# Gate and up blocks of both feed-forward layers: high and low activations in one product of 512 columns

## The chip, the cores and the metric

One core of one Trainium2 chip runs the whole program. The metric is the device time of one execution in microseconds (us). The core has a matrix engine (TensorE; PE in the profile, PEld its weight loads), a vector engine (VectorE, DVE), a scalar engine (ScalarE, ACT), a queue for transfers (SyncE, SP) and eight accumulation banks of 128x512 float32 values (PSUM) that only TensorE's products fill and that VectorE and ScalarE read out.

## The reference, cut to what matters

Two transformer blocks over 256 tokens of width 1024. The second one has two feed-forward layers of this form, with D_FF = 2816:

```
def swiglu(x, w_gate, w_up, w_down):
    return (jax.nn.silu(x @ w_gate) * (x @ w_up)) @ w_down

h = h + 0.5 * swiglu(rms_norm(h, ffn1_norm[i]), ffn1_w_gate[i], ffn1_w_up[i], ffn1_w_down[i])
...
h = h + 0.5 * swiglu(rms_norm(h, ffn2_norm[i]), ffn2_w_gate[i], ffn2_w_up[i], ffn2_w_down[i])
```

Everything else (the first block with its expert layer, the attention and retention branches of the second, the last gate) is not touched by the change.

## The kernel before, in words

All data is float32, but TensorE is fed rounded numbers of the type fp32r. So each operand is held as a high part and a low part: `wh` and `wl` for weights, `hh` and `hl` for activations (`yh` and `yl` for the activations of the down products). A product of two such operands is three matmuls (`mm3`, line 529): high times high, then the low activations against the high weights, then the high activations against the low weights, all added up in the same bank. The weights are the stationary operand and 256 tokens are the moving one.

The weights come in chunks of 128x2048 values (1 MB), each in two units of 128x1024. ScalarE makes the high part of a unit (`wh`, line 1233), VectorE the low part (`wl`, line 1803). There are six slots for units (`NU`), so a unit may be split once TensorE has used the one six units before it. Both engines split a fixed distance ahead of the work (`AHEAD` = 4 units, in the helper `ahead`), and do it in the order of their written-out programs.

Each feed-forward layer runs over eleven column blocks i of 256. Called g, u and d here, they go over TensorE in the order g0 u0 g1 f1a u1 g2 u2 d0 d1 g3 u3 d2 ... g10 u10 d9 d10 in the first layer (`f1a` is a sum for a norm) and g0 u0 s2 g1 u1 d0 g2 u2 d1 ... in the second (`s2` is such a sum too). A block g, u or d is 16 triples of matmuls. g and u each fill one bank (`lin_fm`); the two 128x256 halves of the bank are two groups of 128 columns m. d adds into banks 4 to 7 over all i (`down_fm`).

On VectorE, `ffn_act` (line 2253) multiplies g by the token scale `rs` out of its bank (L2257), waits for ScalarE's silu (L1521), multiplies with u out of its bank (L2262), multiplies by the scale once more (L2264); ScalarE rounds the result to `yh` (L1507), VectorE makes `yl` (L1823). Both engines then split further weights.

Which bank a result goes to is fixed beforehand by a table (`job`, `over`, `fixed_to`). `take` on TensorE waits until every earlier result of that bank has been read out:

```
        def take(pe, name):
            p, b, n = jobs[name]
            if n:
                pe.wait_ge(bank_out[p][b], n)
            return BK[b]
```

In the first layer g0 is in bank 4, u0 in 5, `f1a` in 3, and g1, u1, g2, u2, g3, ... take the banks 0, 1, 2, 3, 0, ... in turn. In the second layer g0, u0, g1, u1, ... take the banks 0, 1, 2, 0, ... in turn, and `s2` is in bank 3.

Between the blocks VectorE has other work of its own in the first layer: the scales out of `f1a` ahead of `ffn_act(0)`, a norm (`first_normed`, L2296) after `ffn_act(4)`, and the tables of angles (`rope_tables`, L2300 to L2319) ahead of `ffn_act(5)`, for which ScalarE takes two sines (L1552, L1554).

Of the kernel before, what the change touches and what calls it, by code (L numbers as in the profile page):

```python
# [12 lines left out]
def offsets(pairs):  # L13
# [13 lines left out]
ohe rank tm tm_h flag pg g32 moe  # L27
g_gx g_gc g_pt g_s g_tr g_d g_yh g_sc
hn_h f1x f1_s f1_t f1_yh f1_yl f1_yb tab
rot rope ix_mm ix_sel sco  # L30
rs_mm rv_mm rm_mm rm_sq rvar yn
at_mm at_m at_e at_d at_tr at_v at_yh
iw_t av_t sgy rg_l mg mg_h mg_l
# [19 lines left out]
    "unscaled_l": [("f1_l", 8), ("mx_l", 8), ("f2_l", 8), ("pl_l", 8)],  # L53
    "gated_h": [("rg_h", 4), ("gain", 8)],
    "norm_t": [("n2_t", 8), ("hn_t", 8)],
}


# [3 lines left out]
def program(nc, D, out):  # L62
# [5 lines left out]
    ALU, ACT, AX = mybir.AluOpType, mybir.ActivationFunctionType, mybir.AxisListType  # L68
    cx = ExitStack()

    with cx:
# [16 lines left out]
        def S(name):  # L88
            return sems[name]

        def nth(name, n):
            return sems[name], base[name] + n
# [5 lines left out]
        RAW = [sb(f"raw{i}", [128, 2048]) for i in range(NR)]  # L98
        with ExitStack() as outer:
            ob = lambda name, n: outer.enter_context(nc.sbuf_tensor(name, [128, n], f32r))  # L100
            HHt, HLt = ob("hh", 4096), ob("hl", 4096)
            WH = [ob(f"wh{i}", 1024) for i in range(NU)]
            WL = [ob(f"wl{i}", 1024) for i in range(NU)]
        XGt = []
# [9 lines left out]
        wide = lambda T: T[:, :].rearrange("p (k t) -> p k t", k=8)  # L114
        half = lambda T, i: T[:, 2048 * i:2048 * i + 2048].rearrange("p (k t) -> p k t", k=8)
        HW, LW = wide(HHt), wide(HLt)
        HX, LX = HW[:, :, 0:256], LW[:, :, 0:256]
        HC, LC = HW[:, :, 256:512], LW[:, :, 256:512]
        H0, L0, H1, L1 = half(HHt, 0), half(HLt, 0), half(HHt, 1), half(HLt, 1)
        YH, YHA = YHt[:, 0:2048].rearrange("p (k t) -> p k t", k=8), YHt[:, 2048:3072].rearrange("p (k t) -> p k t", k=4)  # L120
        YL, YLA = YLt[:, 1024:3072].rearrange("p (k t) -> p k t", k=8), YLt[:, 0:1024].rearrange("p (k t) -> p k t", k=4)
# [20 lines left out]
        two = lambda b: b[:, :].rearrange("p (k t) -> p k t", k=2)  # L142
# [103 lines left out]
        chunks, where = [], {}  # L246
# [122 lines left out]
        def done(e, name, i=0):  # L369
            e.wait_ge(*nth("used", units_used(2 * where[name, i] + 1)))  # L370

        jobs, uses = {}, {"": [0] * 8, "g_": [0] * 8, "d_": [0] * 8}
# [6 lines left out]
        def over(pool, p=""):  # L379
            at = [0]  # L380

            def put(*names):
                for n in names:
                    job(n, pool[at[0] % len(pool)], p)
                    at[0] += 1
            return put
# [12 lines left out]
        def fixed_to(banks, *names):  # L399
            fixed(*zip(names, banks))  # L400
# [10 lines left out]
        rot = over([5, 6, 7], "g_")  # L411
# [28 lines left out]
        rot = over([0, 1, 2, 3])  # L440
        job(("f1", "g", 0), 4)
        job(("f1", "u", 0), 5)
        job("f1a", 3)
        for i in range(1, 11):
            rot(("f1", "g", i), ("f1", "u", i))
        for i in range(4):
            job(("f1", "y", i), 4 + i)
        put = over(ALL7)
# [33 lines left out]
        put = over(ALL7)  # L482
        job("s2", 3)
        put(*[("wo2", i) for i in range(4)])
        rot = over([0, 1, 2])
        for i in range(11):
            rot(("f2", "g", i), ("f2", "u", i))
        for i in range(4):
            job(("f2", "y", i), 4 + i)
        put = over(ALL7)  # L490
# [6 lines left out]

        def bank(name):
            return BK[jobs[name][1]]

        def copied(name):
            p, b, n = jobs[name]
            return bank_out[p][b]

        def evicted(e, name):
            p, b, n = jobs[name]
            e.wait_ge(bank_out[p][b], n + 1)
# [7 lines that stand above are left out]
        def tensor_program(pe):  # L515
# [18 lines left out]
            def lin_fm(c, outs, xh, xl, ready=None, nk=8, ncols=256, N=256, between=None):  # L534
                per, hk = 512 // N, nk // 2
                for u in range(2):
                    if u and between:
                        between()
                    h, l = weights(2 * where[c] + u, hk)
                    for m in range(ncols // 128):  # L540
                        o = outs[m // per][:, (m % per) * N:(m % per) * N + N]
                        for k in range(hk):
                            x = u * hk + k
                            if ready and m == 0:
                                pe.wait_ge(*nth(ready[0], ready[1][x]))
                            t = mm3(o, h[:, k, m * 128:(m + 1) * 128], l[:, k, m * 128:(m + 1) * 128], xh[:, x, :], xl[:, x, :],
                                    x == 0 and m % per == 0, x == nk - 1)
                    t.then_inc(S("used"), 1)

            def lin_tm(c, outs, ntt, xh, xl, ready=None, ncols=256):  # L550
# [29 lines left out]
            up_to = list(range(1, 9))  # L580
# [26 lines left out]
            for x in range(2):  # L607
                b = take(pe, ("cb", x))
                for k in range(4):
                    t = mm(b[:, k * 128:k * 128 + 128], CV[:, 4 * x + k, 0:1].broadcast_to([128, 128]), ident, k == 0, True)  # L610
                t.then_inc(S("cb"), 1)
            ada_rows(0)
            b = take(pe, "statx")
# [5 lines left out]
            b = take(pe, "statc")  # L619
# [25 lines left out]
            for j in range(4):  # L645
                b = take(pe, ("dec", j))
# [145 lines left out]
            b = take(pe, "w_stat")  # L792
# [4 lines left out]
            b = take(pe, "router")  # L797
            arrived(pe, where["w_r", 0])
            w = RAW[raw_of[where["w_r", 0]]][:, 0:288].rearrange("p (k n) -> p k n", k=8)
            for k in range(8):  # L800
                pe.wait_ge(*nth("n2_h", k + 1))
                for x in range(2):
                    t = mm(b[:, 256 * x:256 * x + 36], H2F[:, k, 128 * x:128 * x + 128], w[:, k, :], k == 0 and x == 0, k == 7)
            t.then_inc(S("used"), 2)
            for x in range(2):
                for q in range(2):
                    b = take(pe, ("tm", x, q))
                    for k in range(4):
                        t = pe.transpose(b[:, k * 128:(k + 1) * 128], H2F[:, 4 * q + k, x * 128:x * 128 + 128], ident)
                    t.then_inc(S("tm"), 1)  # L810
            b = take(pe, "rank")
# [207 lines left out]
            b = take(pe, "f1a")  # L1019
# [3 lines left out]
            mm(b[:, 256:512], ones, ACCB, False, True).then_inc(S("f1a_mm"), 1)  # L1023
            lin_fm(("f1u", 1), [take(pe, ("f1", "u", 1))], H0, L0)
            for i in range(2, 11):
                lin_fm(("f1g", i), [take(pe, ("f1", "g", i))], H0, L0)
                lin_fm(("f1u", i), [take(pe, ("f1", "u", i))], H0, L0)
                if i == 2:
                    down_fm("f1", "f1d", 0, 11, ("f1_yl", "f1_yb"))
                down_fm("f1", "f1d", i - 1, 11, ("f1_yl", "f1_yb"))  # L1030
# [135 lines left out]
                lin_fm(("w_out2", i), [take(pe, ("wo2", i))], H0, L0, ("mg_l", [1, 1, 2, 2, 3, 3, 4, 4]) if i == 0 else None)  # L1166

            for i in range(11):
                lin_fm(("f2g", i), [take(pe, ("f2", "g", i))], H1, L1, ("f2_l", up_to) if i == 0 else None)
                lin_fm(("f2u", i), [take(pe, ("f2", "u", i))], H1, L1)  # L1170
                if i == 0:
                    stat_sum("s2", "s2_acc", "s2_mm")
                else:
                    down_fm("f2", "f2d", i - 1, 11, ("f2_yl", "f2_yb"))
# [13 lines left out]
            for m in range(2):  # L1188
                f = slice(m * 128, m * 128 + 128)
                b = take(pe, ("pg", 3 + m))  # L1190
# [28 lines left out]
        def scalar_program(a):  # L1219
# [282 lines left out]
            def split_act(i, P, dn, ready, T):  # L1502
                ready()
                if i >= 2:
                    done(a, dn, i - 2)
                y = 4 * (i % 2)
                a.activation(YH[:, y:y + 2, :], T[i % 2], ACT.Copy).then_inc(S(P + "_yh"), 1)  # L1507
# [9 lines left out]
            assert at[0] == after  # L1517

            def silu_scaled(i, P, G):
                evicted(a, (P, "g", i))  # L1520
                a.activation(G[i % 2], G[i % 2], ACT.Silu).then_inc(S(P + "_s"), 1)  # L1521

            def ffn_act(i, P, dn, G, T):
                silu_scaled(i, P, G)
                split_act(i, P, dn, lambda: a.wait_ge(*nth(P + "_t", i + 1)), T)

            through("f1u", 0)
# [263 lines left out]
        def vector_program(v):  # L1791
# [23 lines left out]
            def step(ins):  # L1815
                ins.then_inc(S(own[0]), 1)
                own[1] += 1

            def prev():
                v.wait_ge(*nth(own[0], own[1]))  # L1820
# [430 lines left out]
            assert at[0] == after and own[1] == stepped  # L2251

            def ffn_act(i, P, G, T, rs, g, u):
                done(v, g, i)
                if i >= 2:
                    evicted(v, (P, "u", i - 2))
                v.tensor_tensor(G[i % 2], two(bank((P, "g", i))), rs, ALU.mult).then_inc(copied((P, "g", i)), 1)  # L2257
                v.wait_ge(*nth(P + "_s", i + 1))
                done(v, u, i)
                if i >= 2:  # L2260
                    v.wait_ge(*nth(P + "_yl", i - 1))
                v.tensor_tensor(T[i % 2], G[i % 2], two(bank((P, "u", i))), ALU.mult).then_inc(copied((P, "u", i)), 1)  # L2262
                evicted(v, (P, "u", i))
                v.tensor_tensor(T[i % 2], T[i % 2], rs, ALU.mult).then_inc(S(P + "_t"), 1)  # L2264
                low_act(i, P, T)

# [521 lines left out]
```

## Time and profile before

| | |
|---|---|
| median of 3 runs | 1176.04 us (1169.3 to 1182.11) |
| the profiled execution | 1174.52 us, of which the span of instructions is 1172.6 us |
| granted TensorE clock, mean | 0.971 |
| busy: TensorE, weight loads | 1101.8 us (94%), 937.3 us (80%) |
| busy: VectorE, ScalarE | 709.0 us (60%), 519.4 us (44%) |

The shares are means over the whole span, over stages with different limits. A matmul's record covers its whole way through the array, so that records overlap: the distance from start to start is what one costs in a stream. PEclk of 1.00 is the full clock of 2.4 GHz, 0.50 is 1.2 GHz.

### The profile page before, as it was taken

The numbers are of one execution on the slowest core, as the hardware profiler recorded it, in microseconds if no ns is written. First come the engines' busy times: TensorE is split into PE (matmuls) and PEld (weight loads), VectorE is DVE, ScalarE is ACT, GpSimd is POOL, SyncE is SP. The second block draws the span as 40 slices with busy tenths as digits, with TensorE's granted clock in tenths as the row PEclk, the third lists the DMA queues.
The fourth block names the chain that finished last, engine by engine and source line by source line (L and its number), as shares of the span: only waits on it lengthen the run. The fifth ranks groups of instructions, "written<-read, shape, count | busy, mean of one in ns | idle before, by whom it ended". The sixth has DMA issues, their size and how long they took to land.

```text
span 1172.6 us, 18961 instructions
## 1 busy us (share of the span) xinstructions
PE 1101.8 (94%) x7908; PEld 937.3 (80%) x7908; DVE 709.0 (60%) x1125; ACT 519.4 (44%) x797; POOL 0.2 (0%) x4
## 2 busy tenths in 40 slices
PE   5899997899999998999999989978999999999997
PEld 3689876545555554999999988877889999999996
DVE  1879777423332335876756789767645776555667
ACT  3674223211111113654434576358854554443455
POOL 0000000000000000000000000000000000000000
PEclk9899997799999999999999999988999999999998
DMA  9945617999999947465454433432345545545321
GB/s 384 379 164 216 252 60 292 388 422 413 408 410 406 407 189 325 146 246 182 180 205 162 148 108 125 146 108 73 108 144 203 197 168 202 182 173 201 134 98 36
DMA packets 38153, 257.72 MB, mean 220 GB/s; under 512 B 4368, under 2 KB 5264, under 8 KB 7856
## 3 DMA queue, kind: packets, MB, share of 16 engines
q1 hardware_dynamic: 36720, 252.38, 56.4%
q10 hardware_dynamic: 1344, 4.08, 0.9%
q8 instruction: 65, 1.06, 0.4%
q14 instruction: 24, 0.20, 0.0%
HBM read 255.39 MB, written 1.05 MB: 219 GB/s over the span
## 4 chain that ended last, share of the span: by engine, by line
PE 67%; DVE 11%; ACT 5%; issue 2%; DVEq 0%; ACTq 0%
PE bank L527 66%; DVE wl L1803 3%; ACT wh L1233 2%; DVE rstd L1827 1%; DVE xt L1853 1%; ACT arena L1578 1%; DVE acc L1865 1%; DVE hl L1870 0%; PE bank L903 0%; ACT L1243 0%; ACT arena L1243 0%; PE bank L861 0%; DVE tn L1885 0%; DVE arena L2021 0%; ACT rstd L1247 0%
## 5 line engine op out<-in xcount | busy, mean ns | idle before, releaser
L527 PE MATMUL bank<-hh,wh 128*128 128x256 f32 (+2 forms) x1256 | 365.0, 291 | 9.6 <-DVE hl L1823 4.3
L527 PE MATMUL bank<-hl,wh 128*128 128x256 f32 (+2 forms) x1256 | 360.4, 287 | 0.0
L527 PE MATMUL bank<-hh,wl 128*128 128x256 f32 (+2 forms) x1256 | 360.1, 287 | 0.0
L1803 DVE TENSOR_TENSOR wl<-raw,wh 128x1024 fp32r<-128x1024 f32 (+4 forms) x238 | 267.7, 1164 | 82.6 <-ACT wh L1233 79.2
L1233 ACT ACTIVATE wh<-raw 128x1024 fp32r<-128x1024 f32 (+4 forms) x238 | 227.9, 1003 | 71.3 <-PE bank L527 71.2
L527 PEld LDWEIGHTS bank<-hh,wh 128*128 128x128 f32 (+1 forms) x1256 | 242.5, 193 | 18.9 <-issue 13.6
L527 PEld LDWEIGHTS bank<-hl,wh 128*128 128x128 f32 (+1 forms) x1256 | 242.7, 193 | 1.3
L527 PEld LDWEIGHTS bank<-hh,wl 128*128 128x128 f32 (+1 forms) x1256 | 242.6, 193 | 1.2
L527 PE MATMUL bank<-yh,wh 128*128 128x256 f32 x512 | 147.3, 288 | 4.7 <-DVE yl L1823 3.1
L527 PE MATMUL bank<-yl,wh 128*128 128x256 f32 x512 | 145.9, 285 | 0.0
L527 PE MATMUL bank<-yh,wl 128*128 128x256 f32 x512 | 145.7, 285 | 0.0
L527 PEld LDWEIGHTS bank<-yh,wh 128*128 128x128 f32 x512 | 99.3, 194 | 6.5 <-DVE yl L1823 3.3
L527 PE MATMUL bank<-arena 64*128 64x256 f32 (+6 forms) x404 | 94.5, 413 | 9.3 <-DVE arena L2364 4.5
L527 PEld LDWEIGHTS bank<-yl,wh 128*128 128x128 f32 x512 | 99.2, 194 | 0.5 <-issue 0.5
L527 PEld LDWEIGHTS bank<-yh,wl 128*128 128x128 f32 x512 | 99.3, 194 | 0.0
L527 PE MATMUL bank<-raw,xg 128*64 128x512 f32 (+1 forms) x352 | 85.3, 578 | 3.5 <-ACT xg L1417 3.5
L527 PEld LDWEIGHTS bank<-arena 64*128 64x128 f32 (+3 forms) x404 | 55.0, 184 | 35.8 <-issue 21.4
L1243 ACT ACTIVATE arena<-bank 128x512 f32<-128x512 f32 (+4 forms) x79 | 40.4, 531 | 72.5 <-PE bank L527 68.1
L2196 DVE SCALAR_TENSOR_TENSOR arena<-arena,bank 128x256 f32<-128x256 f32 x16 | 7.7, 481 | 106.1 <-ACT arena L1464 106.1
L527 PEld LDWEIGHTS bank<-raw,xg 128*64 128x64 f32 (+1 forms) x352 | 31.0, 154 | 48.9 <-issue 48.8
L1464 ACT ACTIVATE arena<-bank 128x256 f32<-128x256 f32 x16 | 6.2, 385 | 108.7 <-PE bank L527 108.7
L527 PE MATMUL bank<-raw,arena 128*64 128x512 f32 (+1 forms) x240 | 49.3, 538 | 1.1 <-DVE yl L2187 1.1
(273 smaller groups left out, 1374.3 us busy)
## 6 DMA issues: line engine op xcount, KB each, us to landing
raw<-in_gu SPq DMA_DIRECT2D x40, 1024.0 KB, 11.0
arena<-in_gu SPq DMA_DIRECT2D x24, 1024.0 KB, 9.3
raw<-in_gd SPq DMA_DIRECT2D x22, 1024.0 KB, 8.0
raw<-in_w_adt SPq DMA_DIRECT2D x14, 1024.0 KB, 6.1
raw<-in_f1g SPq DMA_DIRECT2D x11, 1024.0 KB, 4.9
raw<-in_f1d SPq DMA_DIRECT2D x11, 1024.0 KB, 4.8
raw<-in_f2g SPq DMA_DIRECT2D x11, 1024.0 KB, 4.8
raw<-in_f2u SPq DMA_DIRECT2D x11, 1024.0 KB, 4.8
```

Of the source, the lines that this page charges most:

```text
L527: return pe.matmul(o, l, m, start=start, stop=stop, skip_group_check=True)
L1233: a.activation(WH[slot_of[U]][:, 0:n], src, ACT.Copy).then_inc(S("wh"), 1)
L1243: a.activation(dst, src, fn).then_inc(copied(name), 1)
L1464: a.activation(SLT[p % 2], bank(("gu", p))[:, 0:256], ACT.Silu).then_inc(S("g_s"), 1)
L1578: t = a.activation(A[p:p + half, 0:n, :], T[q:q + half, 0:n, :], ACT.Copy)
L1803: v.tensor_tensor(WL[slot_of[U]][:, 0:n], src, WH[slot_of[U]][:, 0:n].bitcast(f32), ALU.subtract).then_inc(S("wl"), 1)
L1827: step(v.reciprocal(RS[:, :], RS[:, :]))
L1853: t = v.scalar_tensor_tensor(XT[:, k, :], b, s, XT[:, k, :], ALU.mult, ALU.add)
L1865: v.tensor_tensor(ACC[:, :], ACC[:, :], SQ[k % 2][:, :], ALU.add).then_inc(S(acc), 1)
L2196: v.scalar_tensor_tensor(HSL[p % 2], SLT[p % 2], GC[:, p:p + 1], bank(("gu", p))[:, 256:512], ALU.mult, ALU.mult).then_inc(copied(("gu", p ...
```

## The change

The high and low activations `hh` and `hl` become two halves of one tensor, and a view `HL` gives, for a block of 128 rows x, both parts as 2x256 columns. For the g and u blocks 2 to 10 of the first layer and 1 to 10 of the second, `lin_wide` multiplies the high weights once with these 512 columns, and the low weights with the 256 high columns. Two matmuls stand where three stood. Each group m of 128 columns now fills a whole bank: its first half holds high weights by high activations plus low weights by high activations, the second half high weights by low activations. The two halves are added when they are read out: ScalarE copies the second half to SBUF (128x256 each), VectorE adds the first half to it. A block g needs two banks, a block u two more. The scale is then applied in SBUF.

```
-        for i in range(1, 11):
-            rot(("f1", "g", i), ("f1", "u", i))
+        rot(("f1", "g", 1), ("f1", "u", 1))
+        for i in range(2, 11):
+            fixed_to([2, 3, 0, 1], ("f1", "g", i, 0), ("f1", "g", i, 1), ("f1", "u", i, 0), ("f1", "u", i, 1))
...
-        rot = over([0, 1, 2])
-        for i in range(11):
-            rot(("f2", "g", i), ("f2", "u", i))
+        fixed_to([0, 1], ("f2", "g", 0), ("f2", "u", 0))
+        for i in range(1, 11):
+            fixed_to([2, 3, 0, 1], ("f2", "g", i, 0), ("f2", "g", i, 1), ("f2", "u", i, 0), ("f2", "u", i, 1))
...
+            def lin_wide(c, name, i):
+                outs = [take(pe, name + (m,)).rearrange("p (s t) -> p s t", s=2) for m in range(2)]
+                for u in range(2):
+                    h, l = weights(2 * where[c] + u, 4)
+                    for m, o in enumerate(outs):
+                        f = slice(m * 128, m * 128 + 128)
+                        for k in range(4):
+                            x = 4 * u + k
+                            mm(o, h[:, k, f], HL[:, i, x], x == 0, False)
+                            t = mm(o[:, 0, :], l[:, k, f], HL[:, i, x, 0], False, x == 7)
                     t.then_inc(S("used"), 1)
...
             def silu_scaled(i, P, G):
-                evicted(a, (P, "g", i))
+                if is_wide(P, i):
...
+                    for m in range(2):
+                        a.activation(G[i % 2][:, m, :], two(bank((P, "g", i, m)))[:, 1, :], ACT.Copy).then_inc(S(P + "_w"), 1)
+                    a.wait_ge(*nth(P + "_g", j + 1))
...
                 a.activation(G[i % 2], G[i % 2], ACT.Silu).then_inc(S(P + "_s"), 1)
...
+                def whole(name, out, n):
+                    for m in range(2):
+                        v.wait_ge(*nth(P + "_w", n + m + 1))
+                        b = two(bank(name + (m,)))
+                        v.tensor_tensor(out[:, m, :], out[:, m, :], b[:, 0, :], ALU.add).then_inc(copied(name + (m,)), 1)
+                    for m in range(2):
+                        evicted(v, name + (m,))
...
+                if wide:
+                    whole((P, "g", i), G[i % 2], 4 * j)
+                    v.tensor_tensor(G[i % 2], G[i % 2], rs, ALU.mult).then_inc(S(P + "_g"), 1)
...
+                if wide:
+                    whole((P, "u", i), T[i % 2], 4 * j + 2)
+                    v.wait_ge(*nth(P + "_s", i + 1))
+                    step(v.tensor_tensor(T[i % 2], T[i % 2], G[i % 2], ALU.mult))
+                    prev()
```

`ffn_act` of ScalarE likewise copies the second halves of u before `yh`.

## Rows read from the trace of the kernel before

**Rows 1.** The page: span, busy TensorE, and a ScalarE read of a 128x256 half bank

```profile
span 1172.6 us, 18961 instructions
PE 1101.8 (94%) x7908; PEld 937.3 (80%) x7908; DVE 709.0 (60%) x1125; ACT 519.4 (44%) x797; POOL 0.2 (0%) x4
...
L1464 ACT ACTIVATE arena<-bank 128x256 f32<-128x256 f32 x16 | 6.2, 385 | 108.7 <-PE bank L527 108.7
```

**Rows 2.** Windows, both layers: length, PE, PEld, DVE, ACT, POOL busy (count), PEclk, DMA share, GB/s

```profile
518.00:659.60 141.60, 141.60 (x1183) 141.60 (x1182) 92.63 (x106) 62.09 (x70) 0.00 (x0) 1.00 0.51 188
924.90:1128.90 204.00, 204.00 (x1700) 203.95 (x1700) 124.06 (x140) 92.97 (x113) 0.00 (x0) 1.00 0.48 173
```

**Rows 3.** The chain that ended last, the same two stretches: start, us, what

```profile
517.55 142.09 PE bank L527 x1182
...
924.88 204.07 PE bank L527 x1699
```

**Rows 4.** Timeline of TensorE in the first layer, 256 columns: start, us

```profile
645.78 0.28 PE L527 MATMUL bank<-hh,wh 128*128 128x256 f32 x1
645.90 0.28 PE L527 MATMUL bank<-hl,wh 128*128 128x256 f32 x1
...
646.14 0.28 PE L527 MATMUL bank<-hh,wh 128*128 128x256 f32 x1
```

**Rows 5.** Timeline of TensorE, 512 columns at full clock; five matmuls left out between

```profile
46.62 0.39 PE L527 MATMUL bank<-hh,wh 128*128 128x512 f32 x1
...
47.98 0.39 PE L527 MATMUL bank<-hh,wh 128*128 128x512 f32 x1
```

**Rows 6.** Timeline of TensorE: first matmuls of u2 and d0, last of d1, g3

```profile
499.70 0.28 PE L527 MATMUL bank<-hh,wh 128*128 128x256 f32 x1
...
505.46 0.28 PE L527 MATMUL bank<-yh,wh 128*128 128x256 f32 x1
...
516.86 0.28 PE L527 MATMUL bank<-yh,wl 128*128 128x256 f32 x1
517.55 0.36 PE L527 MATMUL bank<-hh,wh 128*128 128x256 f32 x1 [0.41 <-DVE wl L1803]
```

**Rows 7.** Timeline of VectorE: a 128x256 operation on a bank, u1's reading, next weights

```profile
490.69 0.42 DVE L2280 TENSOR_TENSOR arena<-bank,rstd 128x256 f32<-128x256 f32 x1
...
506.38 0.69 DVE L2262 TENSOR_TENSOR arena<-arena,bank 128x512 f32<-128x512 f32 x1 [0.70 <-ACT arena L1521]
...
516.17 8.04 DVE L1803 TENSOR_TENSOR wl<-raw,wh 128x1024 fp32r<-128x1024 f32 x7 [0.26 <-ACT wh L1233]
```

**Rows 8.** Timeline of TensorE at one restart; windows right after two restarts

```profile
40.32 0.76 PE L527 MATMUL bank<-hh,wh 128*128 128x512 f32 x1 [3.82 <-DVE hl L1823]
...
40.30:46.30 6.00, 5.98 (x14) 4.74 (x15) 4.86 (x11) 6.00 (x12) 0.00 (x0) 0.50 1.03 397
...
783.50:790.40 6.90, 6.82 (x25) 5.47 (x26) 5.50 (x6) 2.52 (x7) 0.00 (x0) 0.50 0.44 152
```

**Rows 9.** Timelines around `ffn_act(5)`: VectorE, ScalarE's last sine, TensorE's g6

```profile
559.23 1.23 DVE L1803 TENSOR_TENSOR wl<-raw,wh 128x1024 fp32r<-128x1024 f32 x1 [0.56 <-ACT wh L1233]
...
566.89 0.68 DVE L2257 TENSOR_TENSOR arena<-bank,arena 128x512 f32<-128x512 f32 x1
...
571.34 6.90 DVE L1803 TENSOR_TENSOR wl<-raw,wh 128x1024 fp32r<-128x1024 f32 x6 [0.26 <-ACT wh L1233]
...
567.01 0.63 ACT L1554 ACTIVATE arena<-arena 128x512 f32<-128x512 f32 x1 [1.48 <-DVE arena L2319]
...
569.46 0.28 PE L527 MATMUL bank<-hh,wh 128*128 128x256 f32 x1
```

**Rows 10.** Timelines at g1 of the second layer: TensorE, ScalarE's reading of `s2`

```profile
952.20 0.47 PE L527 MATMUL bank<-hh,wh 128*128 128x256 f32 x1
...
952.59 0.47 ACT L1247 ACTIVATE rstd<-bank,small 128x256 f32<-128x256 f32 x1 [3.21 <-PE bank L527]
```

**Rows 11.** Timelines at the end of the first layer: `yl` of block 10, d10

```profile
652.47 0.69 DVE L1823 TENSOR_TENSOR yl<-arena,yh 128x512 fp32r<-128x512 f32 x1 [0.70 <-ACT yh L1507]
...
655.86 0.28 PE L527 MATMUL bank<-yh,wh 128*128 128x256 f32 x1
```

More of the change, by code:

```diff
@@ L29 @@
 hn_h f1x f1_s f1_t f1_yh f1_yl f1_yb tab
-rot rope ix_mm ix_sel sco
+ix_mm ix_sel sco
 rs_mm rv_mm rm_mm rm_sq rvar yn
@@ L55 @@
     "norm_t": [("n2_t", 8), ("hn_t", 8)],
+    "whole": [("f1_g", 9), ("rope", 10), ("f2_g", 10)],
+    "parts": [("f1_w", 36), ("rot", 10), ("f2_w", 40)],
 }
@@ L100, in program @@
             ob = lambda name, n: outer.enter_context(nc.sbuf_tensor(name, [128, n], f32r))
-            HHt, HLt = ob("hh", 4096), ob("hl", 4096)
+            HB = ob("hhl", 8192)
+            HHt, HLt = HB[:, 0:4096], HB[:, 4096:8192]
             WH = [ob(f"wh{i}", 1024) for i in range(NU)]
@@ L118, in program @@
         HC, LC = HW[:, :, 256:512], LW[:, :, 256:512]
+        HL = HB[:, :].rearrange("p (s i k t) -> p i k s t", s=2, i=2, k=8)
         H0, L0, H1, L1 = half(HHt, 0), half(HLt, 0), half(HHt, 1), half(HLt, 1)
@@ L499, in bank, with is_wide @@
             return BK[jobs[name][1]]
+        def is_wide(P, i):
+            return (P, "g", i, 0) in jobs
         def copied(name):
@@ L547, in lin_fm @@
                                     x == 0 and m % per == 0, x == nk - 1)
+                    t.then_inc(S("used"), 1)
+            def lin_wide(c, name, i):
[8 more added lines that the diff above has]
+                            t = mm(o[:, 0, :], l[:, k, f], HL[:, i, x, 0], False, x == 7)
                     t.then_inc(S("used"), 1)
@@ L1025, in tensor_program @@
             for i in range(2, 11):
-                lin_fm(("f1g", i), [take(pe, ("f1", "g", i))], H0, L0)
-                lin_fm(("f1u", i), [take(pe, ("f1", "u", i))], H0, L0)
+                lin_wide(("f1g", i), ("f1", "g", i), 0)
+                lin_wide(("f1u", i), ("f1", "u", i), 0)
                 if i == 2:
@@ L1168, in tensor_program @@
             for i in range(11):
-                lin_fm(("f2g", i), [take(pe, ("f2", "g", i))], H1, L1, ("f2_l", up_to) if i == 0 else None)
-                lin_fm(("f2u", i), [take(pe, ("f2", "u", i))], H1, L1)
+                if i:
+                    lin_wide(("f2g", i), ("f2", "g", i), 1)
+                    lin_wide(("f2u", i), ("f2", "u", i), 1)
+                else:
+                    lin_fm(("f2g", 0), [take(pe, ("f2", "g", 0))], H1, L1, ("f2_l", up_to))
+                    lin_fm(("f2u", 0), [take(pe, ("f2", "u", 0))], H1, L1)
                 if i == 0:
@@ L1519, in silu_scaled @@
             def silu_scaled(i, P, G):
-                evicted(a, (P, "g", i))
+                if is_wide(P, i):
+                    j = i - 2 if P == "f1" else i - 1
+                    done(a, P + "g", i)
+                    if i >= 2:
+                        a.wait_ge(*nth(P + "_t", i - 1))
+                    for m in range(2):
+                        a.activation(G[i % 2][:, m, :], two(bank((P, "g", i, m)))[:, 1, :], ACT.Copy).then_inc(S(P + "_w"), 1)
+                    a.wait_ge(*nth(P + "_g", j + 1))
+                else:
+                    evicted(a, (P, "g", i))
                 a.activation(G[i % 2], G[i % 2], ACT.Silu).then_inc(S(P + "_s"), 1)
@@ L1524, in ffn_act @@
                 silu_scaled(i, P, G)
+                if is_wide(P, i):
+                    done(a, P + "u", i)
+                    if i >= 2:
+                        a.wait_ge(*nth(P + "_yl", i - 1))
+                    for m in range(2):
+                        a.activation(T[i % 2][:, m, :], two(bank((P, "u", i, m)))[:, 1, :], ACT.Copy).then_inc(S(P + "_w"), 1)
                 split_act(i, P, dn, lambda: a.wait_ge(*nth(P + "_t", i + 1)), T)
@@ L2253, in ffn_act @@
             def ffn_act(i, P, G, T, rs, g, u):
+                wide = is_wide(P, i)
+                j = i - 2 if P == "f1" else i - 1
+                def whole(name, out, n):
[3 more added lines that the diff above has]
+                        v.tensor_tensor(out[:, m, :], out[:, m, :], b[:, 0, :], ALU.add).then_inc(copied(name + (m,)), 1)
+                    for m in range(2):
+                        evicted(v, name + (m,))
                 done(v, g, i)
                 if i >= 2:
-                    evicted(v, (P, "u", i - 2))
-                v.tensor_tensor(G[i % 2], two(bank((P, "g", i))), rs, ALU.mult).then_inc(copied((P, "g", i)), 1)
-                v.wait_ge(*nth(P + "_s", i + 1))
+                    v.wait_ge(*nth(P + "_t", i - 1))
+                if wide:
+                    whole((P, "g", i), G[i % 2], 4 * j)
+                    v.tensor_tensor(G[i % 2], G[i % 2], rs, ALU.mult).then_inc(S(P + "_g"), 1)
+                else:
+                    v.tensor_tensor(G[i % 2], two(bank((P, "g", i))), rs, ALU.mult).then_inc(copied((P, "g", i)), 1)
+                if not wide:
+                    v.wait_ge(*nth(P + "_s", i + 1))
                 done(v, u, i)
@@ L2261, in ffn_act @@
                     v.wait_ge(*nth(P + "_yl", i - 1))
-                v.tensor_tensor(T[i % 2], G[i % 2], two(bank((P, "u", i))), ALU.mult).then_inc(copied((P, "u", i)), 1)
-                evicted(v, (P, "u", i))
+                if wide:
+                    whole((P, "u", i), T[i % 2], 4 * j + 2)
+                    v.wait_ge(*nth(P + "_s", i + 1))
+                    step(v.tensor_tensor(T[i % 2], T[i % 2], G[i % 2], ALU.mult))
+                    prev()
+                else:
+                    v.tensor_tensor(T[i % 2], G[i % 2], two(bank((P, "u", i))), ALU.mult).then_inc(copied((P, "u", i)), 1)
+                    evicted(v, (P, "u", i))
                 v.tensor_tensor(T[i % 2], T[i % 2], rs, ALU.mult).then_inc(S(P + "_t"), 1)
```

## The prediction

> **What bounds the kernel now.** The page comes first: over the span TensorE is busy 94% [rows 1], but its records overlap, so this alone doesn't say that it is the limit. The windows over the two feed-forward layers do: 141.6 us with TensorE busy all the time at full clock, and 204.0 us likewise, while VectorE is busy 65% and 61% of them and the DMA engines about half [rows 2]. The chain of waits agrees: in each layer it stays on TensorE for one unbroken piece of 142.09 and 204.07 us [rows 3]. In these stretches time is what TensorE's instructions cost, each about 0.120 us from start to start. Outside them, in the first 30 us after the first layer's norm sum, VectorE runs a long serial chain, and TensorE has work only because it need not wait for it.
>
> **What a merged triple saves.** Matmuls of 256 columns start 0.12 us apart [rows 4]: a triple costs 0.36. Matmuls of 512 columns at full clock take (47.98 - 46.62) / 6 = 0.2267 us [rows 5]. Now 256 columns at 2.4 GHz are 0.1067 us and 512 are 0.2133, so in both rows a matmul costs its columns plus 0.0133. The columns stay 768 per triple; one instruction goes. The pair costs 0.2267 + 0.12 = 0.3467, and 0.0133 us is saved. A block has 16 triples, so g and u of one i save 32 x 0.0133 = 0.427 us. Nine i in the first layer: 3.84; ten in the second: 4.27; together 8.1 us, or 0.7%. That is all there is to gain. The weight loads are also one fewer per triple, but they run beside the matmuls [rows 1, 2] and I give them no further gain.
>
> The Trainium skill ("TensorE: Matmul & The Clock Gate", "Wait — 56ns, not 53.3ns?") puts this fixed cost per warm matmul at about 2.5 ns. By that rule the 608 merged triples would save 1.5 us instead of 8.1. The trace shows 13.3 ns for both widths, and it decides.
>
> The rows of 512 columns read one run of 512; the new product reads two runs of 256 from two places. No row shows that. I take the cost of the second run as nothing, since the first value of a run is all that differs; the upper bound is that each run pays the 0.0133 of a matmul of its own, which is then no saving at all. A gain beyond the columns is excluded, as the array takes one column per clock in both rows.
>
> **The banks at u2 of the first layer.** Here lies the largest term. Before, u2 went to bank 3; now its groups take banks 0 and 1, where g1 and u1 are, and `take` waits for both before u2's first matmul. VectorE reads u1 at 506.38 for 0.69 us, thus until 507.07 [rows 7]. It can't do so earlier: it has run without a longer wait since the norm sum, through its two reciprocals, the weights and ffn_act(0). None of that is changed. TensorE began u2 at 499.70 [rows 6], and would be there 0.21 us earlier, as g2 is merged. It now starts at about 507.15: it idles 7.66 us, and u2 begins 7.45 us later than before. Merged u2 gives back 0.21. Before, TensorE waited between d1 and g3 for weights, 517.55 - (516.86 + 0.12) = 0.57 us [rows 6]. Of that nothing remains: VectorE starts those weights at 516.17 [rows 7]. In the new order ffn_act(2) ends later, at about u2's end (512.7) plus 4 us of reading and splitting, and the weights of g3 follow by 519, while g3 isn't due until after 524. So the term is 7.45 - 0.21 - 0.57 = 6.67 us.
>
> After such a pause the clock is not whole. TensorE idled 3.82 us and began again at 40.32, and the clock granted was 0.50 for the 6.0 us that followed; after another pause of 4.5 us it was 0.50 for 6.9 us [rows 8]. At 1.2 GHz the same work takes twice as long, so half of such a stretch is lost: 3.0 us by the first, 3.45 by the second. I take 3.0, and as ends 3.5 and 1.5, the latter for half rate that lasts half as long as in the shorter row. The Trainium skill ("TensorE: Matmul & The Clock Gate", "Part 1: The HAM clock gate") has half rate as the state that idling brings back; the trace agrees. Together the place costs 9.7 us.
>
> **VectorE's tables ahead of ffn_act(5).** The new evictions lengthen the path from the end of u to the next weights. Two copies of 0.385 [rows 1] and two additions of 0.42 [rows 7], in turns, stand where one reading of 0.69 stood, and the product with G comes on top; the additions overlap the copies, so the path grows by some 1.2 us per i. In an ordinary i this costs nothing: VectorE waits several us for TensorE. Two such waits cover it at the layer's end also: yl of block 10 is ready at 652.47 + 0.69 = 653.16, wanted at 655.86 [rows 11], so 2.7 us of cover against 1.2. But at i = 5 the wait is only 0.56 us [rows 9]; first_normed has eaten the rest. So rope_tables starts about 0.65 late. The last sine ended at 567.64 [rows 9], now 568.3; two copies and the last addition bring 568.3 + 0.77 + 0.42 = 569.5 until banks 2 and 3 are free. Merged g5 and u5 want g6 at 569.46 - 0.42 = 569.04 [rows 9]: 0.45 us of wait, where before g6 had another bank. Then u6's weights: from the free banks, scale 0.69, silu 0.63, copies of u 0.77, last addition 0.42, two products 1.38, yh 0.63, yl 0.69 and gaps of some 0.3 give 575.0, and 1.2 us for the first low unit 576.2. TensorE would begin u6 at 569.5 + 5.55 = 575.05. That is 1.2 us more, 1.6 in all. Its ends are 0 and 3.
>
> **The norm sum of the second layer.** s2 is in bank 3, and g1 now needs bank 3. Before, g1 ran on at 952.20, while ScalarE read s2 from 952.59 to 953.06 [rows 10]. So g1 waits until about 953.1: 0.9 us. u1 then wants banks 0 and 1; u0 is read by 957.3, u1 begins at 958.65, so there is no second u2 here. The silu's table load comes after the reading and isn't in the way.
>
> **What costs nothing.** VectorE gains four additions of 0.42 per i, 1.7 us of a period of 16.85, being now at 65% [rows 2]; ScalarE four copies, 1.5 us, at 44%. The cover is their waits for TensorE; without it a late unit would stop TensorE for as long as it is late. The new waits on ScalarE (done u, then the copies) have yh and later weights queued behind them, and yh needed u before too. The layout of `hh` and `hl` moves nothing else, and the transfers run half empty.
>
> **The sum.** First layer: 9.67 for the place of u2, which holds the saving of i = 2, -3.41 for the other eight i, +1.6 for the tables: +7.9. Second: -4.27 + 0.9 = -3.4. Net +4.5 us. The profiled execution of 1174.52 us would become 1179.0; it lies 1.5 under the median of the runs, and the median would become 1176.04 + 4.5 = 1180.5. A measurement of this kernel tells about 1% (11.8 us) from nothing. This is within it.
>
> **Rivals.**
> *The place of u2 costs little.* If TensorE were let into banks 0 and 1 in time, the rest is -8.1 + 0.9 + 1.6 = -5.6, hence 1170.4. For it: u1 itself is finished by 493.9 (499.70 less g2's 5.76), long before, so a small change in VectorE's order would be enough. Against it: the change makes none, the wait is on the count of readings of each bank, and the row of u1's reading is plain. Chance 0.10.
> *Two runs cost as two matmuls.* The place is every merged product; the price is 608 x 0.0133 = 8.1 us, so +12.6 in all and 1188.6, slower by over 1%. It decides from a distance of 0.239 us between a 512-column matmul and its follower, where the merging gives back only 0.8 us; at 0.2267 my sum holds. For it: nothing in the trace reads two runs at this width. Against: nothing shows a cost for it either. Chance 0.11.
> *ScalarE and VectorE hand over too slowly in every i.* Six handovers per i stand where two stood. yl(10) comes 3.06 us after u10's end (650.1, 5.76 before d10), two units of 1.2 bring the weights of the next u by 5.5, and a next u would want them 11.3 after (d and g): 5.8 us ahead [rows 11]; the delay must grow from 1.2 to over 5.8 for TensorE to wait each time. If it did by 0.5 us in each of 18 periods: +9, 1189. Chance 0.07.
> *The fixed cost is the page's 2.5 ns.* Then the gain is 1.5, and with 12.6 of losses the time 1187.1. Both rows at full clock say otherwise; chance 0.02.
>
> The forecast keeps 0.70, with its own range of 1176 to 1184, from the ends of the clock (1.5 to 3.5) and of the tables (0 to 3) and some for the spread of runs. For 8 in 10 the range takes in most of both rivals: 1170 to 1189. A gain over 1% (under 1164.3) would ask for more than the 8.1 us there are; 0.03. Slower by over 1% (over 1187.8) are the two-run case, the handovers and a bit of the forecast's tail: 0.19. Within 1%: 0.78.
>
> **What the changed profile would show.** Right, if 512-column matmuls in ffn stretches start 0.227 us apart and pairs 0.347; if there is an idle of 7 to 8 us on TensorE ahead of u2, released by VectorE's reading of u1, followed by a clock of 0.5; if periods from g3 on are 16.85 us instead of 17.28; if g6 and u6 wait 1 to 2 us together; if g1 of the second layer waits 0.9 us for ScalarE. Wrong, if the pairs take 0.36, if a wait recurs in each period, or if the pause at u2 isn't there.

## The result, and the profile after

The changed kernel takes 1180.84 us (median of 20 runs) where the kernel before takes 1174.89 (20 runs): ratio 1.005, with a 95% interval of 1.0039 to 1.0062. That is 5.9 us slower (4.6 to 7.3). Forecast was +4.5, on top of the 1176.04 us that three runs had given: 1180.5.

First the page of the changed kernel: the span, and the busy time of the engines.

```profile
span 1176.1 us, 17972 instructions
PE 1098.1 (93%) x7300; PEld 905.9 (77%) x7300; DVE 736.3 (63%) x1201; ACT 540.1 (46%) x873; POOL 0.2 (0%) x4
```

Against [rows 1] there are exactly 608 matmuls and 608 weight loads fewer, and the two other engines have 27 and 21 us more to do. Whether that costs anything the page can't say. The windows over most of the two layers (columns as in [rows 2]):

```profile
524.10:668.00 143.90, 142.56 (x946) 130.22 (x944) 103.98 (x142) 69.79 (x102) 0.00 (x0) 1.00 0.50 185
969.00:1134.00 165.00, 165.00 (x1105) 151.48 (x1104) 110.98 (x145) 81.19 (x120) 0.00 (x0) 1.00 0.48 176
```

In the second layer TensorE is still never without work, at full clock; VectorE is busy 67% where it was 61% [rows 2]. In the first, 1.3 us are missing to TensorE even past g3. The list of who waited for whom, TensorE's part, from the norm sum to the layer's end (us in total, times, longest):

```profile
PE bank L535 <- issue: 7.6, 2, 7.4
PE bank L535 <- DVE wl L1842: 1.2, 1, 1.2
```

One wait of 7.4 us stands out. "issue" means that the profile knew no releaser for it; the time line names it. TensorE at the start of u2 is the first row here, VectorE's reading of u1 (L2323, L2262 before) the second:

```profile
504.62 0.76 PE L535 MATMUL bank<-hhl,wh 128*128 128x512 f32 x1 [7.42 <-issue]
...
503.83 0.69 DVE L2323 TENSOR_TENSOR arena<-arena,bank 128x512 f32<-128x512 f32 x1 [0.70 <-ACT arena L1554]
```

And the windows on u2:

```profile
504.70:509.60 4.90, 4.90 (x15) 4.19 (x16) 3.95 (x6) 3.06 (x5) 0.00 (x0) 0.50 0.85 348
509.70:512.50 2.80, 2.80 (x18) 2.43 (x17) 0.91 (x2) 0.63 (x1) 0.00 (x0) 1.00 0.76 243
```

u1 is read until 504.52, and u2 starts 0.10 later: the wait on the bank, as forecast. From the last start of g2 it is 7.69 us. Then come 4.9 us at a granted clock of 0.50, and u2 takes 7.96 us from its first start to d0's, where 16 pairs at full clock take 5.65. The wait ahead of g3 is gone:

```profile
523.98 0.28 PE L535 MATMUL bank<-yh,wl 128*128 128x256 f32 x1
524.10 0.40 PE L535 MATMUL bank<-hhl,wh 128*128 128x512 f32 x1
```

These stand 0.12 apart, against 0.69 in [rows 6]. Now a steady period of the first layer, and inside it single matmuls (time line of TensorE; rows of g at the starts of i = 4 and 5, then of a later block):

```profile
541.16 0.40 PE L535 MATMUL bank<-hhl,wh 128*128 128x512 f32 x1
...
558.22 0.40 PE L535 MATMUL bank<-hhl,wh 128*128 128x512 f32 x1
...
611.12 0.40 PE L535 MATMUL bank<-hhl,wh 128*128 128x512 f32 x1
611.35 0.28 PE L535 MATMUL bank<-hhl,wl 128*128 128x256 f32 x1
611.47 0.40 PE L535 MATMUL bank<-hhl,wh 128*128 128x512 f32 x1
...
612.18 0.40 PE L535 MATMUL bank<-hhl,wh 128*128 128x512 f32 x1
```

The period is 17.06 us, not 16.85. Three pairs take 612.18 - 611.12 = 1.06, so a pair costs 0.3533 and not 0.3467. A merged triple saves 6.7 ns instead of the 13.3 read from [rows 4, 5]. This is the largest miss in size. It isn't the same everywhere, though. In g1 and u1 of the second layer the same alternation, also at a granted clock of 1.00, runs as forecast; there three pairs take 962.88 - 961.84 = 1.04 us, so a pair costs 0.3467:

```profile
961.84 0.39 PE L535 MATMUL bank<-hhl,wh 128*128 128x512 f32 x1
...
962.88 0.39 PE L535 MATMUL bank<-hhl,wh 128*128 128x512 f32 x1
```

These two blocks take 11.17 us, those of every later i of that layer 11.31.

The two small waits are there. Around the tables of angles, VectorE's additions for g5 and first weights after ffn_act(5), then TensorE's first matmuls of g6 and of u6:

```profile
574.77 0.75 DVE L2300 TENSOR_TENSOR arena<-arena,bank 128x256 f32<-128x256 f32 x2 [1.07 <-ACT arena L1550]
...
581.30 6.90 DVE L1842 TENSOR_TENSOR wl<-raw,wh 128x1024 fp32r<-128x1024 f32 x6 [0.26 <-ACT wh L1257]
...
575.62 0.47 PE L535 MATMUL bank<-hhl,wh 128*128 128x512 f32 x1 [0.17 <-issue]
...
582.67 0.47 PE L535 MATMUL bank<-hhl,wh 128*128 128x512 f32 x1 [1.17 <-DVE wl L1842]
```

g6 starts 0.10 after the additions end at 575.52, u6 0.14 after the first low weights (1.24 us of the row at 581.30). And at g1 of the second layer, which begins when ScalarE has read `s2` (952.20 and 952.59 in [rows 10]):

```profile
957.38 0.47 ACT L1271 ACTIVATE rstd<-bank,small 128x256 f32<-128x256 f32 x1 [3.21 <-PE bank L535]
...
957.95 0.47 PE L535 MATMUL bank<-hhl,wh 128*128 128x512 f32 x1 [0.61 <-issue]
```

From the first matmul of u1 to the last of d10, the first layer takes 182.50 us where it took 173.50; the second, from s2 to d10, 177.36 where it took 178.86. Together +7.5. The medians of the executions say +5.9, and their interval ends at 7.3. The stretch between the layers, which the change doesn't touch, took 288.8 us in this profile and 290.5 in the one before. All of that is one short piece of it, in which the granted clock was 0.50 before and 1.00 after (the windows, before and then after):

```profile
735.80:739.20 3.40, 3.40 (x11) 2.84 (x12) 3.16 (x12) 0.73 (x2) 0.00 (x0) 0.50 0.86 306
742.20:745.70 3.50, 3.50 (x25) 3.35 (x26) 3.26 (x12) 1.98 (x3) 0.00 (x0) 1.00 0.83 300
```

Up to there the starts of TensorE's instructions agree to 0.02 us, and past it they differ by 1.65. TensorE had idled for 1.8 us just ahead of this piece in both. Of the profiles of the experiments below, which all have this idling, three (e_warm, e_order8, e_start3) have the slow piece too. What decides it no run shows. The repeated executions point the same way: of the changed kernel's 20, the shortest (1176.19 us) had a mean granted clock of 0.972, the longest (1185.06) 0.968. So spans aren't compared below, only the layers themselves and the medians.

### The profile page after: what moved, and what is told of

Same layout as the page of the kernel before. It is cut to its first block, busy times and chain, and to the rows that moved or that the text cites. A ratio compares the mean times of both kernels' runs of the same rounds, so it can differ in the third digit from the quotient of the medians.

```text
span 1176.1 us, 17972 instructions
## 1 busy us (share of the span) xinstructions
PE 1098.1 (93%) x7300; PEld 905.9 (77%) x7300; DVE 736.3 (63%) x1201; ACT 540.1 (46%) x873; POOL 0.2 (0%) x4
## 4 chain that ended last, share of the span: by engine, by line
PE 38%; DVE 7%; ACT 4%; issue 2%; DVEq 0%; ACTq 0%
PE bank L535 38%; DVE wl L1842 2%; ACT wh L1257 1%; DVE rstd L1866 1%; ACT arena L1617 1%; DVE acc L1904 1%; DVE xt L1892 0%; DVE hhl L1909 0%; ACT L1267 0%; ACT arena L1267 0%; DVE tn L1924 0%; ACT arena L1675 0%; DVE small L2491 0%; DVE arena L2563 0%; DVE arena L2488 0%
## 5 line engine op out<-in xcount | busy, mean ns | idle before, releaser
L535 PE MATMUL bank<-hhl,wh 128*128 128x256 f32 (+2 forms) x1904 | 468.9, 329 | 18.4 <-issue 8.2
L535 PEld LDWEIGHTS bank<-hhl,wh 128*128 128x128 f32 (+1 forms) x1904 | 322.9, 193 | 57.4 <-issue 23.5
L535 PE MATMUL bank<-hhl,wl 128*128 128x256 f32 (+2 forms) x1256 | 360.2, 287 | 0.0
L535 PEld LDWEIGHTS bank<-hhl,wl 128*128 128x128 f32 (+1 forms) x1256 | 242.3, 193 | 1.2
L535 PE MATMUL bank<-wh,hhl 128*128 128x256 f32 x320 | 61.7, 293 | 1.8 <-DVE wl L1842 1.8
L535 PEld LDWEIGHTS bank<-wh,hhl 128*128 128x128 f32 x320 | 52.6, 200 | 3.4 <-issue 3.3
L2300 DVE TENSOR_TENSOR arena<-arena,bank 128x256 f32<-128x256 f32 x76 | 28.5, 417 | 42.2 <-ACT arena L1563 41.2
```

The lines of the kernel that those rows point to most:

```text
L535: return pe.matmul(o, l, m, start=start, stop=stop, skip_group_check=True)
L2300: v.tensor_tensor(out[:, m, :], out[:, m, :], b[:, 0, :], ALU.add).then_inc(copied(name + (m,)), 1)
```

## The experiments

Ratios are to the kernel before, run on the same chip.

**1. Is the pause the bank's alone?** The kernel before, products unmerged, with u2 put where u1 is:

```
-        for i in range(1, 11):
-            rot(("f1", "g", i), ("f1", "u", i))
+        rot(("f1", "g", 1), ("f1", "u", 1))
+        for i in range(2, 11):
+            fixed_to([2, 1], ("f1", "g", i), ("f1", "u", i))
```

> The kernel before with its three products, only that from i = 2 on the first layer has g in bank 2 and u in bank 1, so that u2 stands in the bank of u1. Theory (the pause at u2 is the bank's alone): TensorE idles 7.4 us ahead of u2, until VectorE has read u1, then runs at a granted clock of 0.5 for some 4 to 6 us; +7.4 - 0.6 + 2.3 = +9.1 us, ratio 1.008. Rival (the pause comes from the new evictions or their waits): no pause, ratio 1.000.

Measured: ratio 1.0069 (1.0048 to 1.0091); the first layer takes 181.92 us, 8.4 more than before. TensorE at u2, and VectorE's reading of u1:

```profile
508.40 0.58 PE L528 MATMUL bank<-hh,wh 128*128 128x256 f32 x1 [7.27 <-DVE arena L2263]
...
507.66 0.69 DVE L2263 TENSOR_TENSOR arena<-arena,bank 128x512 f32<-128x512 f32 x1 [0.70 <-ACT arena L1522]
```

No product is merged here, and no eviction is new, and yet nearly the whole loss is there, 8.4 of the 9.1 us that u2's banks cost the changed kernel (experiment 5), this time with its releaser's name. The rival falls.

**2. What is the clock's share?** The changed kernel, with the pause filled (each of the 30 products is two matmuls in the trace):

```
                 lin_wide(("f1g", i), ("f1", "g", i), 0)
+                if i == 2:
+                    for _ in range(30):
+                        mm(BK[7][:, 0:128], ones, ones, True, True)
                 lin_wide(("f1u", i), ("f1", "u", i), 0)
```

> The changed kernel with 30 products of the constant ones into bank 7 on TensorE between g2 and u2, whose sums nothing reads (d0 starts that bank anew). They fill most of the pause. Theory (the clock's share of the loss is a separate 2.3 us): u2 starts at the same distance behind VectorE's reading of u1, the granted clock stays 1.0, u2 takes 5.65 instead of 7.96 us; 2.3 us under the changed kernel, ratio 1.003. Rival (the slow u2 isn't due to the pause): u2 stays at 7.96 us, ratio 1.005.

Measured: ratio 1.0039 (1.002 to 1.0057). The windows on the fill and on u2:

```profile
499.90:507.50 7.60, 6.93 (x62) 6.74 (x60) 5.75 (x8) 3.26 (x5) 0.00 (x0) 1.00 0.44 153
507.50:513.10 5.60, 5.56 (x32) 4.93 (x33) 4.54 (x7) 3.07 (x5) 0.00 (x0) 1.00 0.80 320
```

The clock stays at 1.00, and u2 takes 5.63 us instead of 7.96. The first layer takes 180.15, 2.35 less. The medians move the same way, though their intervals overlap. So u2 loses 2.3 us by the clock in this profile, where 3.0 was taken. The loss isn't fixed: after the same pause u2 takes 7.30 us in e_contig's profile, 7.23 in e_near's and 7.13 in e_flat's (experiment 3), a loss of 1.5 to 1.7 us.

**3. Why does a pair cost 0.3533?** My theory after the result was the second run of 256 columns, the unknown that the prediction had bounded. Three layouts test it. The low activations right behind the high ones (e_contig), two runs at half the distance (e_near), and one plain run in the program as well (e_flat):

```
-        HL = HB[:, :].rearrange("p (s i k t) -> p i k s t", s=2, i=2, k=8)
-        H0, L0, H1, L1 = half(HHt, 0), half(HLt, 0), half(HHt, 1), half(HLt, 1)
+        HL = HB[:, :].rearrange("p (i k s t) -> p i k s t", s=2, i=2, k=8)
+        H0, L0, H1, L1 = (HL[:, i, :, s, :] for i in range(2) for s in range(2))
```

(e_near: `"p (i s k t) -> p i k s t"`; e_flat: e_contig with `mm(o[:, :], h[:, k, f], HC2[:, i, x, :], ...)`, where HC2 has the 512 columns as one dimension.)

> The changed kernel with the low activations of each block of 128 rows right behind the high ones, so that the 512 columns are one run. Theory (a second run costs 6.7 ns): the product of 512 columns falls from 0.2333 to 0.2267 us, a pair from 0.3533 to 0.3467, the period of the first layer from 17.06 to 16.85 us, the whole 4.1 us under the changed kernel, about 1.0015 of the kernel before. Rival (a 512-column product followed by one of 256 costs more, whatever it reads): 0.3533 and 17.06 stay, 1.005 stays.

> The changed kernel with two runs still, but 2048 values apart instead of 4096. If the break between the runs costs, whatever the distance: pair 0.3533 us. If the distance costs: below 0.3533, perhaps 0.350. If neither: as in the run with one run of 512.

> The changed kernel with the low activations behind the high ones and both the read and the written 512 columns given as one plain run in the program. If the earlier run with adjacent parts still read two runs, and a second run costs 6.7 ns: pair 0.3467 us, period 16.85. If runs cost nothing: pair 0.3533, period 17.06, as before.

Measured: e_contig 1.0077 (1.0048 to 1.0106); the other two were run once, 1180.64 and 1182.75 us. TensorE at the start of a g in e_contig, then in e_near, then in e_flat:

```profile
595.52 0.40 PE L535 MATMUL bank<-hhl,wh 128*128 128x512 f32 x1
595.75 0.28 PE L535 MATMUL bank<-hhl,wl 128*128 128x256 f32 x1
595.87 0.40 PE L535 MATMUL bank<-hhl,wh 128*128 128x512 f32 x1
...
596.58 0.40 PE L535 MATMUL bank<-hhl,wh 128*128 128x512 f32 x1
```

```profile
596.52 0.40 PE L535 MATMUL bank<-hhl,wh 128*128 128x512 f32 x1
...
597.58 0.40 PE L535 MATMUL bank<-hhl,wh 128*128 128x512 f32 x1
```

```profile
614.92 0.40 PE L536 MATMUL bank<-hhl,wh 128*128 128x512 f32 x1
...
615.98 0.40 PE L536 MATMUL bank<-hhl,wh 128*128 128x512 f32 x1
```

Three pairs are 1.06 us in each, and the period is 17.07. The theory falls: neither a second run nor its distance costs anything that shows. The medians say nothing against this; e_contig's is above the changed kernel's, though its layers took 0.5 us less. The rival is left, a product of 512 columns next to one of 256: the rows of [rows 5] had neighbours of their own width. It was tested next.

**4. Does the change of width cost?** Only the order inside a unit of weights is new: eight products of 512, then eight of 256 (e_order8), or in fours (e_order4):

```
+                    for part in range(2):
+                        for m, o in enumerate(outs):
+                            f = slice(m * 128, m * 128 + 128)
+                            for k in range(4):
+                                x = 4 * u + k
+                                if part == 0:
+                                    mm(o, h[:, k, f], HL[:, i, x], x == 0, False)
+                                else:
+                                    t = mm(o[:, 0, :], l[:, k, f], HL[:, i, x, 0], False, x == 7)
```

> The changed kernel with another order inside a unit of weights: first the eight products of 512 columns, then the eight of 256. Theory (each change of width between neighbouring products costs, 6.7 ns a pair of changes): 16 products then take 8 x 0.3467 + 0.0067 = 2.78 us instead of 2.83, a period 16.87 instead of 17.06 us, 608 x 0.0067 x 7/8 = 3.6 us in all: ratio 1.002. Rival (a product of 512 columns costs 0.2333 us in these layers, whoever its neighbour): 17.06 us and 1.005 stay.

> The same in groups of four: four products of 512 columns, then four of 256. Theory (changes of width cost): the distance over a unit lies a quarter of the way back, period 16.85 + 0.05 = 16.90 us. Rival (no change of width costs): 17.06.

Measured in e_order8, TensorE through a unit and a half:

```profile
616.13 2.00 PE L535 MATMUL bank<-hhl,wh 128*128 128x512 f32 x8
617.97 1.11 PE L535 MATMUL bank<-hhl,wl 128*128 128x256 f32 x8
618.92 2.00 PE L535 MATMUL bank<-hhl,wh 128*128 128x512 f32 x8
```

A unit takes 2.79 us instead of 2.83. Eight products of 512 take 1.84, which is 0.027 over 8 x 0.2267; eight of 256 take 0.95, 0.01 under 8 x 0.12. In the trace it is the first five products of 512 after a change that take longer (233, 236, 228, 232 and 231 ns), and from the sixth on they take 227. So in this order a change from 256 to 512 and back costs some 20 ns, once, where the theory had 6.7. In strict alternation the extra is mostly 6.7 ns for each pair. The period is 16.94 us, where 16.87 was expected, and 16.99 in fours, where 16.90 was. The trace thus shows that grouping gains, but only 0.12 and 0.07 us a period where 0.19 and 0.16 were forecast. The medians don't show even that: e_order8 came at 1.0068 (1.0048 to 1.0088), wholly above the 1.002 expected; 18 x 0.12 = 2.2 us less than the changed kernel was due, and four runs of this spread didn't find it. e_order4 was run once (1178.65 us).

Nor is the change of width the cause by itself. In g1 and u1 of the second layer the changed kernel changes width as often as elsewhere and pays nothing for it (0.3467 a pair). In e_contig's, e_near's and e_flat's profiles it is g2 and u2 of that layer that do so, 11.10 us for 32 pairs. What decides between the two rates stays open.

**5. Undo only u2's banks.** Block 2 of the first layer keeps its three products and the banks 2 and 3; the merging starts with block 3:

```
-        rot(("f1", "g", 1), ("f1", "u", 1))
-        for i in range(2, 11):
-            fixed_to([2, 3, 0, 1], ...
+        rot(("f1", "g", 1), ("f1", "u", 1), ("f1", "g", 2), ("f1", "u", 2))
+        for i in range(3, 11):
+            fixed_to([0, 1, 2, 3], ...
```

> The changed kernel with one edit: block 2 of the first layer stays with three products in banks 2 and 3, blocks 3 to 10 are merged in banks 0 to 3. Theory (pause 7.5 and clock 2.3 us are u2's banks alone): no pause at u2, the clock stays 1.0, the 0.6 us wait ahead of g3 comes back; 9.0 us under the changed kernel, ratio 0.998; the waits at g6, u6 and at g1 of the second layer stay. Rival: the pause moves to u3, whose banks 2 and 3 held block 2: 1.005.

Measured: ratio 0.9999 (0.9984 to 1.0015), a bit above the 0.998 that was expected. The first layer takes 173.39 us, 9.1 under the changed kernel; the second 177.37, as in it. There is no pause at u2 or u3, and the old wait ahead of g3 is back:

```profile
519.84 0.47 PE L535 MATMUL bank<-hhl,wh 128*128 128x512 f32 x1 [0.41 <-DVE wl L1846]
```

**6. Undo all three waits.** As above, with s2 in bank 5 and the tables two rounds later:

```
-        job("s2", 3)
+        job("s2", 5)
...
-                if i == 5:
+                if i == 7:
                     rope_tables()
```

> The changed kernel without its three waits: block 2 of the first layer stays with three products and takes banks 2 and 3 as before (blocks 3 to 10 take 0, 1, 2, 3), s2 goes to bank 5, the tables of angles are made ahead of block 7 instead of 5. Theory (the loss is 7.5 of pause, 2.3 of clock, 1.6 of the tables and 0.9 of s2): all four go, and what is left is the merging, 18 blocks x 32 x 0.0067 = -3.9 us less the 0.6 us wait ahead of g3 that was there before: ratio 0.997. Rival (the evictions are the load, and their waits come up elsewhere): at or above 1.000.

Measured: ratio 0.9983 (0.9963 to 1.0002). The layers take 172.58 and 176.52 us, 3.3 under the kernel before. The interval just reaches the rival's 1.000, so that it's the layers that speak against it. One expectation was wrong: u8 still waits.

```profile
613.22 0.28 PE L535 MATMUL bank<-hhl,wl 128*128 128x256 f32 x1
614.30 0.47 PE L535 MATMUL bank<-hhl,wh 128*128 128x512 f32 x1 [0.80 <-DVE wl L1846]
```

g's banks are free in time there, but the weights of the next u are queued on VectorE behind ffn_act, and that behind the tables, in whichever round they stand. So the tables must go behind those weights.

**7. The version that beats both.** e_fix, with the widths grouped, and the tables behind the weights of the next u:

```
+                    for part in (0, 1) if u == 0 else (1, 0):
+                        for m, o in enumerate(outs):
+                            f = slice(m * 128, m * 128 + 128)
+                            for k in range(4):
+                                x = 4 * u + k
+                                if part == 0:
+                                    t = mm(o, h[:, k, f], HL[:, i, x], x == 0, x == 7)
+                                else:
+                                    t = mm(o[:, 0, :], l[:, k, f], HL[:, i, x, 0], False, False)
...
                 ahead("f1d", i - 1)
                 if i == 4:
                     first_normed()
+                if i == 6:
+                    rope_tables()
```

> The kernel of e_fix with two more edits. Inside a block the products of one width stand together, and the second unit starts with those of 256 columns, with which the first ended (eight of 512, sixteen of 256, eight of 512). The tables of angles are made at the end of VectorE's round 6, behind the weights of the next u, instead of ahead of a ffn_act; ScalarE's sines stay ahead of its ffn_act(7). Theory (a change from 256 to 512 costs 20 ns once, and the wait at the tables is u's late weights): a period of 16.91 instead of 17.06 us, no wait of TensorE inside the layers but the 0.6 us ahead of g3; 18 x 0.15 + 1.0 = 3.7 us under e_fix, ratio 0.994. Rival (VectorE has no room for the tables anywhere): the wait moves to d6 or g8, and the ratio stays at 0.996 or above.

Measured: 1166.7 us, ratio 0.9935 (0.9912 to 0.9958). TensorE through one i:

```profile
615.99 2.00 PE L535 MATMUL bank<-hhl,wh 128*128 128x512 f32 x8
617.83 2.08 PE L535 MATMUL bank<-hhl,wl 128*128 128x256 f32 x16
619.74 3.82 PE L535 MATMUL bank<-hhl,wh 128*128 128x512 f32 x16
623.39 2.08 PE L535 MATMUL bank<-hhl,wl 128*128 128x256 f32 x16
625.30 2.00 PE L535 MATMUL bank<-hhl,wh 128*128 128x512 f32 x8
627.15 0.28 PE L535 MATMUL bank<-yh,wh 128*128 128x256 f32 x1
```

And the only wait of TensorE left in the layer, ahead of g3 as before the change:

```profile
PE bank L535 <- DVE wl L1849: 0.4, 1, 0.4
```

g and u of one i take 11.16 us where 96 matmuls took 11.52 before and the alternating pairs mostly 11.31. The layers take 170.56 and 175.21 us, 6.6 under the kernel before in sum, which lies within the interval of the medians (4.9 to 10.3).

## Why the prediction was right

Its verdict and range held, and so did nearly every step. By its own terms:

- *What bounds the kernel.* Right. Only TensorE's instructions, its waits and its clock moved the time. The 27 and 21 us more on VectorE and ScalarE cost at most the 1.65 us at the tables; the pause at u2 and the wait at g1 of the second layer come from where results were placed. All three places were named beforehand.
- *What a merged triple saves.* The term that was mis-sized. Forecast 13.3 ns per triple, 8.1 us in all; it is mostly 6.7 ns, or 608 x 0.0067 = 4.1 us. The step that failed is that "in both rows a matmul costs its columns plus 0.0133", carried over to an alternation of widths. The prediction named the open question as two runs; experiment 3 shows that these cost nothing. Experiment 4 shows that the order of the widths matters, but one pair of blocks in the same trace alternates at the forecast 0.3467, so why most don't stays open. The rule of the Trainium skill weighed beside it ("TensorE: Matmul & The Clock Gate", "Wait — 56ns, not 53.3ns?": a fixed 2.5 ns per warm matmul) would give a saving of 1.5 us. That is nearer to 4.1 than the 8.1 taken from the rows. The trace doesn't bear the rule out all the same: an estimate by it is 0.109 us for a matmul of 256 columns, where [rows 4] have 0.12. The rival that rested on it had 1187.1 us, which didn't come either.
- *The banks at u2.* 7.69 us between starts, of which 0.12 is due, so 7.57 of idling against 7.66 forecast; the wait ahead of g3 vanished as said. Experiments 1 and 5 show that it is the banks alone.
- *The clock after the pause.* 2.3 us (experiment 2) against 3.0, within its ends of 1.5 and 3.5; in the other profiles with this pause it is 1.5 to 2.3. That pausing brings back half rate, as the Trainium skill also has it ("TensorE: Matmul & The Clock Gate", "Part 1: The HAM clock gate"), the trace shows: 0.50 for 4.9 us of u2.
- *The tables.* g6 began 0.45 after the last start where 0.12 is due, u6 1.44: 1.65 us together, 1.6 forecast. The growth of the path after u came out at 1.3 us against 1.2: yl(10) is ready 4.37 us after u10, 3.06 before.
- *The norm sum.* g1 starts 957.95 - 957.85 = 0.10 us after ScalarE has read s2, 0.99 after the last of the sum's products where it was 0.03: 0.96 us more, 0.9 forecast.
- *What costs nothing.* Right: no wait recurs in a steady period, in either layer.

The errors partly cancel: 4.0 us less saved than forecast, 0.7 less lost to the clock. That would make +7.8, and the layers show +7.5, but the medians +5.9 (4.6 to 7.3). The 1.7 us that the slow piece between the layers cost the kernel before would fill the gap of 1.6; but only one execution of each kernel was profiled, so this isn't shown. The closeness is in part luck: the layers miss the +4.5 by 3.0 us, and 1180.5 against 1180.84 looks closer still because the three runs behind 1176.04 lay 1.15 us above the median of twenty.

Of the rivals, the one in which u2's place costs little and the one of handovers that are too slow are out. The one of two runs came out with half of its price, and its mechanism was wrong.

## What to carry to other kernels

When products are merged, look up which bank each wider result takes and when that bank's last tenant is read: here one placement cost more than the whole merging could give, by its wait and by the slow clock after it. Take the cost of a matmul from rows with the order of widths it will have, and keep products of one width together: here that gave 11.16 us for g and u of one i instead of mostly 11.31. A block of work on VectorE that has to go somewhere belongs behind the operands that TensorE needs next, not ahead of them.

## What was not expected of the hardware

A stream of fp32r products of 512 columns runs at 226.7 ns each and one of 256 columns at 120 ns, but alternating they take 353.3 ns a pair in most blocks and 346.7 in a few, though all run the same code. After a change from 256 to 512 in e_order8 the first five take up to 236 ns. Low activations right behind the high ones, half the distance, or one plain run of 512 made no difference to this. After the same 1.8 us of idling between the layers, the granted clock was 0.50 for some 3 us in four of the twelve profiles, at a cost of 1.7 us, and 1.00 in the other eight. VectorE's two additions of 128x256 out of a bank take 0.75 us together, though one alone is 0.42.
